# Start-up loads by token tile, the sine inside the layer loop, and scratch turns on TensorE

## What is computed

```python
for i in range(DEPTH):                                # DEPTH = 2
    h = rms_norm(x, norm_mix_pre[i])
    z = h @ w_in[i]                                   # 1024 x 4384
    c_q, c_kv, k_rope, q_c, k_c, v_c, g_a, g_b, g_c = split(z)
    o_a = mla_attention(c_q, c_kv, k_rope, positions, ...)   # rms_norm(c_q) @ w_uq, rotary by cos/sin(positions * inv_freq)
    o_b = fourier_mix(h)
    o_c = windowed_gqa(q_c, k_c, v_c, positions, gqa_sink[i])  # distances |pq - pk|
    ...                                               # merge, w_out, gated FFN, per-layer embedding
```

## Time and profile before

| | |
|---|---|
| median of 3 runs | 2011.86 us (2010.4 to 2013.39) |
| the profiled execution | 2009.97 us, span 2008.2 us |
| TensorE busy | 1941.9 us, 97% of the span |
| VectorE / ACT / POOL busy | 1101.6 / 953.2 / 185.6 us |
| DMA | 332.71 MB, 166 GB/s on average |

### The profile page before, as it was taken

How to read it: one execution, slowest core, us unless ns; L and a number is a source line. 1 busy time by engine, 2 the same in 40 slices (tenths; PEclk the granted TensorE clock), 3 DMA queues, 4 the chain that set the end, 5 groups by cost and what they waited for, 6 DMA issues and landing times.

```text
span 2008.2 us, 26085 instructions
## 1 busy us (share of the span) xinstructions
PE 1941.9 (97%) x9024; PEld 1563.1 (78%) x9024; DVE 1101.6 (55%) x1326; ACT 953.2 (47%) x1252; POOL 185.6 (9%) x269
## 2 busy tenths in 40 slices
PE   6999999998999999999899999999999999999998
PEld 5777878887777787887788877688878888767886
DVE  5565665556566565545655554554465555555444
ACT  4564454445446445444544444644454444455443
POOL 6310010001421001000100022000011000100000
PEclk9999999999999999999999999999999999999999
DMA  6334465554513555555555553265556554434553
GB/s 202 106 105 152 171 207 188 188 188 138 169 52 120 180 180 189 188 188 172 193 191 187 185 186 126 85 204 188 188 180 198 188 188 167 158 105 147 188 188 105
DMA packets 204827, 332.71 MB, mean 166 GB/s; under 512 B 11328, under 2 KB 150208, under 8 KB 204736
## 3 DMA queue, kind: packets, MB, share of 16 engines
q1 hardware_dynamic: 200368, 319.86, 47.4%
q0 software_dynamic: 3264, 11.54, 1.7%
q10 hardware_dynamic: 1104, 0.16, 0.1%
HBM read 330.47 MB, written 1.05 MB: 165 GB/s over the span
## 4 chain that ended last, share of the span: by engine, by line
PE 59%; issue 32%; DVE 4%; POOL 3%; ACT 2%; DMA 1%; POOLq 0%; ACTq 0%; DVEq 0%
PE ps L501 17%; PE ps L505 17%; PE ps L503 17%; PE ps L664 3%; PE ps L513 2%; PE ps L677 1%; PE ps L700 1%; PE ps L688 1%; DVE wlo L1576 1%; ACT whi L1135 1%; POOL stat L2082 1%; POOL stat L2083 1%; DMA freq<-freq_dram 1%; DVE act_lo L1582 0%; DVE h L1620 0%
## 5 line engine op out<-in xcount | busy, mean ns | idle before, releaser
L1576 DVE TENSOR_TENSOR wlo<-raw,whi 128x2048 fp32r<-128x2048 f32 (+1 forms) x304 | 685.8, 2257 | 542.8 <-ACT whi L1135 542.7
L1135 ACT ACTIVATE whi<-raw 128x2048 fp32r<-128x2048 f32 (+2 forms) x308 | 580.9, 1886 | 437.8 <-PE ps L505 433.7
L501 PE MATMUL ps<-whi,act_hi 128*128 128x512 f32 (+1 forms) x1632 | 619.3, 397 | 16.5 <-DVE act_lo L1582 10.7
L505 PE MATMUL ps<-whi,act_lo 128*128 128x512 f32 (+1 forms) x1632 | 607.1, 389 | 0.0
L503 PE MATMUL ps<-wlo,act_hi 128*128 128x512 f32 (+1 forms) x1632 | 606.2, 389 | 0.0
L501 PEld LDWEIGHTS ps<-whi,act_hi 128*128 128x128 f32 x1632 | 305.6, 189 | 83.4 <-DVE act_lo L1582 11.8
L505 PEld LDWEIGHTS ps<-whi,act_lo 128*128 128x128 f32 x1632 | 307.5, 188 | 64.8
L503 PEld LDWEIGHTS ps<-wlo,act_hi 128*128 128x128 f32 x1632 | 308.3, 189 | 60.0
L1179 ACT ACTIVATE hid<-ps,stat 128x256 f32<-128x256 f32 x132 | 62.6, 475 | 283.5 <-PE ps L513 199.8
L2082 POOL TENSOR_TENSOR stat<-stat,eps 128x1 f32<-128x1 f32 x44 | 32.8, 745 | 1517.5 <-ACT prob L1166 1517.2
L501 PE MATMUL ps<-whi,hid_hi 128*128 128x512 f32 x496 | 153.4, 390 | 0.0
(11 more groups left out here) (205 smaller groups left out, 1801.1 us busy)
## 6 DMA issues: line engine op xcount, KB each, us to landing
raw<-ffn_w_gate_dram SPq DMA_DIRECT2D x88, 512.0 KB, 4.0
raw<-ffn_w_up_dram SPq DMA_DIRECT2D x88, 512.0 KB, 5.0
raw<-ffn_w_down_dram SPq DMA_DIRECT2D x88, 512.0 KB, 3.9
raw<-w_in_dram SPq DMA_DIRECT2D x64, 512.0 KB, 4.4
raw<-w_ffn_gate_dram SPq DMA_DIRECT2D x44, 512.0 KB, 4.0
raw<-w_ffn_up_dram SPq DMA_DIRECT2D x44, 512.0 KB, 5.0
raw<-w_ffn_down_dram SPq DMA_DIRECT2D x44, 512.0 KB, 3.8
raw<-a_w_qkv_dram SPq DMA_DIRECT2D x24, 512.0 KB, 4.4
```

What stands on the lines that cost most here:

```text
L501: nc.tensor.matmul(o, hi, a, start=start, stop=False)
L505: last = nc.tensor.matmul(o, lo, a, start=False, stop=stop)
L1135: nc.scalar.activation(whi[:, u % SLOTS, 0:words], raw[:, u % SLOTS, 0:words], ACT.Copy)\
L1576: nc.vector.tensor_tensor(wlo[:, u % SLOTS, 0:words], raw[:, u % SLOTS, 0:words], whi[:, u % SLOTS, 0:words].bitcast(F32), ALU.subtract)\
```

## The change

- x is loaded in two halves of 128 tokens, tile 0 on SP's queue and tile 1 on ACT's; the first gain row goes ahead of tile 1 on ACT's queue, and the positions behind both. POOL's second gain row is issued after the root of tile 0. The gains' counts in `scaled` and `gained` are adapted.
- ahead of the loop, ACT, VectorE and POOL take tile 0 first and tile 1 when it has landed; POOL's root of tile 1 stands between the steps for the cosine's and for the sine's angles; VectorE's distance steps come last.
- POOL writes the angles to a tile of their own, `angles`; ACT takes their sine in every layer, behind unit 4's rounding; POOL's rotation waits for it.
- TensorE makes 24 scratch turns at the start, turns tile 0, makes 36 more, then enters the loop. At the end of each layer it makes 12 scratch turns, turns tile 0 of the next h, and makes 6 more ahead of the loop's edge. Scratch turns write bank 0 and wait for nothing.

```diff
-WARM_SHORT, WARM_LONG = 8, 12
+WARM_SHORT, WARM_LONG, WARM_FIRST, WARM_START = 6, 12, 24, 36
...
+        angles = sb("angles", [P, 2, T, ROPE // 2])
...
-            sp.dma_start(xs[:, :, :], A["x"][0, :, :].rearrange("(t p) n -> p t n", p=P)).then_inc(s_in["x"], 16)
+            sp.dma_start(xs[:, 0, :], A["x"][0, 0:P, :]).then_inc(s_in["x0"], 16)
...
-            def stay_warm(k, n):
-                free_before("turn", k)
+            def stay_warm(n):
                 for _ in range(n):
-                    nc.tensor.transpose(ps[:, 2 + k % 2, 0:P], ident[:, :], ident[:, :])
+                    nc.tensor.transpose(ps[:, 0, 0:P], ident[:, :], ident[:, :])
...
-                ready, turn_first = rows(TN_MIX, "h_ready", 0, ahead=AHEAD_ONE)
-                turn_first(0)
+                ready = rows(TN_MIX, "h_ready", 0, ahead=AHEAD_ONE, first_turned=True)[0]
...
-                stay_warm(len(TURN1) + TN_MIX, WARM_LONG)
+                stay_warm(WARM_LONG)
+                rows(len(TURN1) + TN_MIX, "h_ready", PER_LAYER["h_ready"])[1](0)
+                stay_warm(WARM_SHORT)
...
             pe.wait_ge(s_ident, 2)
+            w.layer = 0
+            stay_warm(WARM_FIRST)
+            rows(TN_MIX, "h_ready", 0)[1](0)
+            stay_warm(WARM_START)
...
-                split(3)
+                split(1)
+                act.wait_ge(s_setup, ANGLE_STEPS)
+                nc.scalar.activation(cs1[:, :, :, :], angles[:, :, :, :], ACT.Sin).then_inc(sem("trig"), 1)
+                split(2)
...
+            act.dma_start(gains[:, 0, :], A["gains"][0:1, :].partition_broadcast(P).rearrange("p a n -> p (a n)"))\
+                .then_inc(s_in["gain"], 16)
+            act.dma_start(xs[:, 1, :], A["x"][0, P:S, :]).then_inc(s_in["x1"], 16)
             act.dma_start(posk[:, :], ...)
...
-            for t in range(T):
-                square(t, xs[:, t, :])
-            split(1)
+            act.wait_ge(s_in["x0"], 16)
+            square(0, xs[:, 0, :])
             turned_rows_hi(TN_MIX, (0,))
             split(2)
+            act.wait_ge(s_in["x1"], 16)
+            square(1, xs[:, 1, :])
             turned_rows_hi(TN_MIX, (1,))
-
-            act.wait_ge(s_setup, ANGLE_STEPS)
-            nc.scalar.activation(cs1[:, :, :, :], cs1[:, :, :, :], ACT.Sin).then_inc(s_trig, 1)
+            split(1)
...
-            dve.wait_ge(s_in["x"], 16)
-            for t in range(T):
-                gained(0, ht[:, t, :], xs[:, t, :]).then_inc(sem("h_ready"), 1)
+            dve.wait_ge(s_in["gain"], 16)
+            dve.wait_ge(s_in["x0"], 16)
+            nc.vector.tensor_tensor(ht[:, 0, :], xs[:, 0, :], gains[:, 0, :], ALU.mult).then_inc(sem("h_ready"), 1)
+            turned_rows_lo(TN_MIX, 0)
+            dve.wait_ge(s_in["x1"], 16)
+            nc.vector.tensor_tensor(ht[:, 1, :], xs[:, 1, :], gains[:, 0, :], ALU.mult).then_inc(sem("h_ready"), 1)
+            split(2)
+            turned_rows_lo(TN_MIX, 1)
             split(1)
-            turned_rows_lo(TN_MIX, 0)
-            split(2)
...
-            turned_rows_lo(TN_MIX, 1)
             with dve.Fori(0, DEPTH) as li:
...
                 pool.wait_ge(sem("half_read_a"), w.at("half_read_a", 4))
+                pool.wait_ge(sem("trig"), w.at("trig", 1))
...
-            load_gain(0, 0)
-            load_gain(1, 1)
             pool.wait_ge(s_ident, 2)
             w.layer = 0
-            for t in range(T):
-                inverse(t)
+            inverse(0)
+            load_gain(1, 1)
...
             for which in range(2):
+                if which == 1:
+                    inverse(1)
...
-            pool.wait_ge(s_trig, 1)
             with pool.Fori(0, DEPTH) as li:
```

More of the change, by code:

```diff
@@ L122 @@
     q_ready=1, k_ready=1, kc_ready=1, shift=2 * H1, expd=H1, probs=2 * H1, alibi=H1,
-    v_link=34, g_link=16,
+    v_link=34, g_link=16, trig=1,
 )
@@ L320, in two_blocks @@
         landed = [sem(f"landed{s}") for s in range(SLOTS)]
-        s_in = {n: sem(f"in_{n}") for n in ("x", "pos", "const", "mask", "out")}
+        s_in = {n: sem(f"in_{n}") for n in ("x0", "x1", "gain", "pos", "const", "mask", "out")}
         s_setup = sem("setup")
@@ L514, in turn, with rows @@
                 last.then_inc(sem("turn_done"), 1)
-            def stay_warm(k, n):
-                free_before("turn", k)
+            def stay_warm(n):
                 for _ in range(n):
-                    nc.tensor.transpose(ps[:, 2 + k % 2, 0:P], ident[:, :], ident[:, :])
-            def rows(k, name, n, src=None, ahead=AHEAD_TWO):
+                    nc.tensor.transpose(ps[:, 0, 0:P], ident[:, :], ident[:, :])
+            def rows(k, name, n, src=None, ahead=AHEAD_TWO, first_turned=False):
                 src = ht if src is None else src
-                turned = [False, False]
+                turned = [first_turned, False]
                 def turn_tile(t):
@@ L940, in h_rows @@
                 tn += 4
-                return rows(tn - 4, "h_ready", hr - 2, ahead=ahead)
+                return rows(tn - 4, "h_ready", hr - 2, ahead=ahead, first_turned=tn == 4)
             def ffn_here(ready):
@@ L1611, in scaled @@
                 dve.wait_ge(sem("inverse"), w.at("inverse", n + 1))
-                dve.wait_ge(sem(f"gain_in{g % 2}"), w.at(f"gain_in{g % 2}", 16 * (g // 2 + 1)))
+                dve.wait_ge(sem(f"gain_in{g % 2}"), w.at(f"gain_in{g % 2}", 16 * ((g + 1) // 2)))
                 row = gains[:, g % 2, :] if cols is None else gains[:, g % 2, cols[0]:cols[1]]
@@ L2225, in _ @@
                 table(nc.gpsimd.tensor_scalar(near, near, quarter * two_pi, 3.141592, ALU.add, ALU.min))
-                table(nc.gpsimd.tensor_scalar(cs1[:, which], near, -3.141592, None, ALU.max))
+                table(nc.gpsimd.tensor_scalar(angles[:, which], near, -3.141592, None, ALU.max))
             assert n_table[0] == ANGLE_STEPS
```

2 lines of the change are left out of this document (removed).

## The result

The changed kernel took 2015.69 us (median of 17 executions, 2012.64 to 2019.57), the kernel before 2012.05 beside it (median of 17; one of them took 2806.14 us and is not in the ratio). The ratio is 1.0019, 95% interval 1.0011 to 1.0027: within the 0.2% that I had called no change, though the interval lies wholly above 1 and its upper end is beyond 0.2%. I had forecast 2013.8. The profiled execution took 2015.02, its span is 2013.3, 5.1 more than before.

A forecast was written before the change was run, and what follows sets the result against it. TensorE, busy 97% of the span, was taken as the bound, with POOL's chain ending its wait at c = 2; 0.8 + 1.6 - 0.4 = +2.0 us gave 2012.0 profiled, 2013.9 median; recorded 2013.8, range 2008.3 to 2018.0.

The forecast's parts named there:

- The two terms of the head: First layer's start: third w_in column group (c = 2) begins 0.8 us later, then half-clock matmuls cost 1.6 us.
- x and the gain row: Start: half of x and the gain row land near 7 us, weight unit 0 at 12.3, unit 1 about 15.3.
- the rivals of a sooner or a later POOL by queue order: Start: freq lands before 11.6 us (median 2008.4, chance 0.20) or at about 14.4 (median 2018.3, chance 0.20).
- The scratch turns cover from 2 us; first matmul at 16.5: Start: scratch turns run from 2 to about 14 us, so matmuls start near 16.5, 2.1 us sooner, at full clock.
- TensorE waits at c = 1 behind the distance steps: Second w_in column group, first layer: TensorE arrives at 28.8 us and waits until about 30.4 for VectorE's eviction.
- POOL's chain, +0.8: Third w_in column group: POOL's moved root of tile 1 adds 0.81 us, so c = 2 begins at 44.8.
- The clock falls behind the gap, +1.6: After TensorE idles 3.5 us ahead of c = 2, that group runs at 1.2 GHz for a while, costing 1.6 us.
- clock holds: Rival: no clock fall behind the gap at c = 2, or TensorE arrives later; median 2012.3 us, chance 0.15.
- The sine costs nothing: Layer loop: 2.8 us of table loads and sine per layer fit ACT's idle time ahead of unit 5's rounding; cost nothing.
- The layer ends, -0.4: Both layer ends: TensorE's later first matmul is covered or nearly so, a slow stretch may be saved; -0.4 us together.

The follow-up runs named there:

- e1_first0: The changed kernel without the 24 scratch turns ahead of tile 0's turn; 2014.15 us, ratio 1.0009 to the kernel before.
- e7_no_scratch: The changed kernel without any scratch turns in the start; 2013.44 us, ratio 1.0010 to the kernel before.
- e12_after_ffn: The changed kernel with 18 scratch turns ahead of the FFN's second weight unit; 2013.96 us, ratio 1.0004 to the kernel before.
- e6_before_sine: The kernel before with only the angles' sine moved into the layer loop; 2012.11 us, ratio 1.0004.
- e4_before_ends: The kernel before with only the changed layer ends (tile 0's turn and six scratch turns ahead of the loop's edge); 2012.02 us, ratio 0.9995.
- e8_best_old_ends: The changed kernel with old layer ends, POOL's masks behind its roots, distance steps before unit 0's rest, 36 start scratch turns ahead of tile 0's turn; 2015.25 us.
- e11_before_ffn: The kernel before with 18 scratch turns ahead of the FFN's second weight unit; 2008.98 us, ratio 0.9984.
- e2_masks_late: The changed kernel with POOL's six mask steps moved behind roots 2 to 5 of the first layer; 2012.62 us, ratio 1.0002 to the kernel before.

## Why the prediction was right, and where not

*The forecast and its size.* +2.0 us was forecast against the kernel before, +3.6 measured (medians; by the ratio 2.2 to 5.4); the sum itself gives a median of 2013.9, and the 2013.8 on record is 0.1 less. In the profiled executions it was +2.0 against +5.05. Direction and place were right, and so was the last part of the mechanism (POOL's roots hold c = 2, then the clock falls). What makes POOL late was not what I had forecast (below). The two terms of the head, forecast 0.8 + 1.6 = 2.4, measured 1.54 + 1.50 = 3.04; that they come this near is in part luck, since the first was put together from the wrong piece and the second does not come in every execution.

*x and the gain row.* Landed at 6.2 and 6.4, forecast near 7. Right. Unit 0 was there by 11.54 (ACT's rounding in e1_first0), forecast 12.3; unit 1 at 15.79 there and 16.29 in the changed kernel, forecast 15.3. freq, forecast with no shift from 12.4, was there at 12.13: the chain's start at POOL moved by less than 0.3, and the rivals of a sooner or a later POOL by queue order fall. q10 moved 1.19 MB by 12 us, q1 2.07: the byte sum is 3.27 MB against 3.13 before. The Trainium skill (DMA: Bandwidth & Descriptors, section "Issuing engines are not separate DMA queues") says that transfers started by different engines share the 16 DMA engines and that spreading them saves only the time of issue. With 0.14 MB more in the same time, this trace agrees.

*The scratch turns cover from 2 us; first matmul at 16.5.* This step failed. I took TensorE to run from 2 us, as soon as the identity was written; its first instruction came at 6.89 (6.86 by its weight load). So 24 turns at half clock lay over the time in which tile 0's input became ready, and the first matmul came at 18.32. e1_first0, with 15.91, shows that 16.5 was about right for a kernel without those turns, and that it would have been worth 0.87 us at c = 2.

*TensorE waits at c = 1 behind the distance steps.* Forecast 1.6 us, measured 1.72, and 1.76 with the early start. Right, though 1.75 us later in time.

*POOL's chain, +0.8.* Measured +1.54 (root 2 at 39.24 against 37.70), and by another path: this step failed. I let the chain run from freq and added the moved root. But POOL's mask steps read `posf`, which VectorE's distance steps make, and the change puts these last. I had forecast them at 26.8 to 29.6 and asked only what they do to c = 1. They began only at 28.36, behind unit 2's rest, and POOL, done with the angles at 29.1, waited 0.65 us for them. Its masks start at 29.74 instead of 28.70: 1.04 of the 1.54 us. The other 0.50 arise from there to root 2, nearly all in the six mask steps, which took 7.33 us together and before 6.86. The moved root (0.93, as forecast 0.81) and a fifth held step that I had not seen (1.30 instead of about 0.3 us, beside VectorE's product for tile 1 at 14.71) lie ahead of that wait; by this trace a POOL without them would only have waited longer. The wait is not due to tile 0's late turn alone: without the turns ahead of it POOL still waits 0.65 us (e1_first0) and 1.00 us (e7_no_scratch). A kernel with the distance steps moved forward and POOL's masks left where they are was not run.

*The clock falls behind the gap, +1.6.* The gap was 2.24 us and not 3.5, and the clock fell all the same: 17 matmuls in 3.4 us where 29 ran before, +1.50. Right by size. Where TensorE arrives sooner the gap and the stretch at half clock grow (e12_after_ffn). The rival "clock holds" has one execution for it, that of e1_first0, with a gap of 2.24 and no fall in the head: the same gap did both. In four traces with a gap of 2.24 to 3.18 us at c = 2 the clock fell in three.

*The sine costs nothing.* Right, and shown by e6_before_sine. It takes 1.54 us and not 2.8, since no table is loaded back. The load of 1.28 us behind the sine in the kernel before (28.91) was not the sine's: in the changed kernel one stands at 26.10 with no sine before it, and the earlier trace rows has one at 509.13, each ahead of the loop's next rounding. Unit 5's rounding has 1.97 and 2.18 us to spare.

*The layer ends, -0.4.* No cost and no gain was measured (e4_before_ends, and e8_best_old_ends beside e7_no_scratch), but the interval of e4_before_ends, -2.8 to +0.8 us, cannot tell -0.4 from 0. A slow stretch within 15 us behind the first end, which I hoped to save, is there in all five traces with the old order and in six of the nine with the new one. The pause behind the edge is there as forecast, larger (3.83 - 2.06 = 1.8 us against 1.4), and covered.

*What I had not weighed.* The other 2 us of the span's 5.1, and the 1.9 us by which the median of the first three executions lay above the profiled one, fit falls of the clock behind the FFN's second unit, present in one execution and absent in another; e11_before_ffn shows what they are worth. The profile of before happened to have none at either place. A sum made against one such execution can be off by some 1.6 us for each such wait.

## What to carry to other kernels

Before moving an engine's start forward, follow the wait that it meets next to the queue that ends it: here an earlier start and scratch turns on TensorE bought nothing, and the order of six steps on POOL bought 3 us. When steps move to the end of a queue, ask of each result who else waits for it: here POOL's masks waited for VectorE's distance steps. Fill waits of the size seen here (2.6 us) on TensorE with scratch turns that end just before the wait does, but never put them ahead of an instruction whose input may already be there. A moved step must be priced with what it now lies beside: the same POOL step took 0.3 us alone and up to 2.3 beside a long VectorE product in SBUF.

## What was unexpected in the hardware

TensorE's first instruction of a kernel came at 6.76 to 6.89 us in the kernels whose first was a scratch turn with nothing to wait for (e2_masks_late, e8_best_old_ends, e12_after_ffn, the changed kernel), some 5 us after the identity it reads was written.

Behind the edge of its loop TensorE pauses 2.1 to 2.7 us in all nine kernels that have tile 0's turn ahead of the edge (504.25, 504.32 and 499.45 in three of them), and in three of these once more five matmuls later (1.27 us in the changed kernel, 0.52 in e2_masks_late, 1.49 in e12_after_ffn), when nothing waits ahead to hide it.

A wait of 2.24 us at the same matmul was followed by 3.4 us at 1.2 GHz in one kernel and by none in another, a wait of 3.18 by 6.8 us. A wait of 2.6 us in the FFN was followed by a fall in 18 of 22 cases, and with scratch turns in it in none of six. A fall of 3.4 us is worth about 1.5 us, and in this kernel filling two waits took 3.2 us off (e11_before_ffn).
